# Feed-forward layers that multiply tiles without the norm's column factor, and inner tiles in parts of 8, 8 and 6

## The reference, cut to what matters

```
def _rmsnorm(x, g):
    xf = x.astype(jnp.float32)
    y = xf * lax.rsqrt(jnp.mean(xf * xf, axis=-1, keepdims=True) + EPS)
    return (y * g.astype(jnp.float32)).astype(x.dtype)
...
        h = _rmsnorm(x, p['norm_ffn'][l])
        x = x + (jax.nn.silu(h @ p['w_ffn_gate'][l]) * (h @ p['w_ffn_up'][l])) @ p['w_ffn_down'][l]
    y = _rmsnorm(x, p['norm_final'])
```

## Time and profile before

| | before |
|---|---|
| median of 3 runs | 2166.68 us (2166.18 to 2167.81) |
| the profiled execution | 2165.86 us, span 2164.1 us |
| PE busy | 2062.3 us, 95% of the span |
| PEld busy | 1876.2 us, 87% |
| DVE busy | 879.3 us, 41% |
| ACT busy | 430.5 us, 20% |
| POOL busy | 914.9 us, 42% |
| mean granted TensorE clock | 0.979 of full speed |

### The profile page before, as it was taken

The page is one execution under the profiler, slowest core; times in us unless marked ns, Lnnn a source line. Parts: engine busy times, 40 slices in busy tenths (PEclk is TensorE's granted clock), DMA queues, the critical chain, the costliest instruction groups (busy, mean ns, idle before and its releaser), DMA issues.

```text
span 2164.1 us, 33587 instructions
## 1 busy us (share of the span) xinstructions
PE 2062.3 (95%) x13453; PEld 1876.2 (87%) x13453; DVE 879.3 (41%) x1118; ACT 430.5 (20%) x671; POOL 914.9 (42%) x580
## 2 busy tenths in 40 slices
PE   6999999889999999989999999999899999999997
PEld 5999988789999999989998746547498999999996
DVE  4565645552222001359932356555722322210125
ACT  3242333221111000121212322323201111100011
POOL 4333323154454454555553123223454454455443
PEclk9999999899999999999999999999999999999998
DMA  4121212112222222232232474765822122222222
GB/s 172 59 86 60 85 57 84 43 57 78 73 72 78 78 68 78 81 137 75 84 121 75 142 268 145 258 208 186 297 88 78 59 68 77 78 72 75 78 77 88
DMA packets 82071, 224.35 MB, mean 104 GB/s; under 512 B 6352, under 2 KB 11344, under 8 KB 81232
## 3 DMA queue, kind: packets, MB, share of 16 engines
q1 hardware_dynamic: 73344, 202.94, 27.7%
q10 hardware_dynamic: 8656, 20.39, 2.6%
HBM read 170.06 MB, written 53.25 MB: 103 GB/s over the span
## 4 chain that ended last, share of the span: by engine, by line
PE 84%; DVE 8%; DMA 3%; ACT 3%; issue 1%; POOL 1%; DVEq 0%; SPq 0%; ACTq 0%; POOLq 0%
PE psd L210 11%; PE psd L214 11%; PE psd L215 11%; PE psd L211 11%; PE psd L217 11%; PE psd L216 11%; DVE ntmp L284 2%; PE psm L389 2%; PE psm L1314 2%; PE psd L1210 1%; PE psd L1199 1%; DMA c_s<-CsB 1%; PE psd L1136 1%; DMA CsB<-st_c 1%; PE psm L1299 1%
## 5 line engine op out<-in xcount | busy, mean ns | idle before, releaser
L1897 POOL CAST whi<-wraw 128x1024 fp32r<-128x1024 f32 x223 | 236.1, 1059 | 916.6 <-PE psd L217 486.7
L1899 POOL TENSOR_TENSOR wlo<-wraw,whi 128x1024 fp32r<-128x1024 f32 x223 | 540.6, 2424 | 17.9
L210 PE MATMUL psd<-xh,whi 128*128 128x320 f32 x1280 | 406.3, 317 | 19.9 <-ACT xh L257 14.1
L214 PE MATMUL psd<-xl,whi 128*128 128x320 f32 x1280 | 402.7, 315 | 9.5 <-POOL xl L292 7.5
L211 PE MATMUL psd<-xh,whi 128*128 128x320 f32 x1280 | 398.8, 312 | 0.0
L215 PE MATMUL psd<-xl,whi 128*128 128x320 f32 x1280 | 398.8, 312 | 0.0
L216 PE MATMUL psd<-xh,wlo 128*128 128x320 f32 x1280 | 398.5, 311 | 0.0
L217 PE MATMUL psd<-xh,wlo 128*128 128x320 f32 x1280 | 398.3, 311 | 0.0
L210 PEld LDWEIGHTS psd<-xh,whi 128*128 128x128 f32 x1280 | 243.2, 190 | 24.3 <-issue 23.6
L214 PEld LDWEIGHTS psd<-xl,whi 128*128 128x128 f32 x1280 | 242.9, 190 | 17.9 <-POOL xl L292 13.1
L211 PEld LDWEIGHTS psd<-xh,whi 128*128 128x128 f32 x1280 | 243.5, 190 | 0.8 <-issue 0.2
(11 more groups left out here) (378 smaller groups left out, 2902.8 us busy)
## 6 DMA issues: line engine op xcount, KB each, us to landing
wraw<-w SPq DMA_DIRECT2D x224, 512.0 KB, 3.3
CsA<-st_c SPq DMA_DIRECT2D x7, 1024.0 KB, 6.2
CsB<-st_c SPq DMA_DIRECT2D x7, 1024.0 KB, 8.8
c_s<-CsA SPq DMA_DIRECT2D x7, 1024.0 KB, 6.0
c_s<-CsB SPq DMA_DIRECT2D x7, 1024.0 KB, 8.8
z_kept<-zb ACTq DMA_DIRECT2D x16, 320.0 KB, 2.2
ztp<-st_c SPq DMA_DIRECT2D x5, 1024.0 KB, 7.8
CsC<-st_c SPq DMA_DIRECT2D x5, 1024.0 KB, 8.2
```

The source lines that it names most:

```text
L210: pe.matmul(o0, wh, x0, start=st, stop=False)
L214: pe.matmul(o0, wh, l0, start=False, stop=False)
L1897: pool.tensor_copy(whi[s][:], wraw[s][:]).then_inc(w_high, 1)
L1899: pool.tensor_tensor(wlo[s][:], wraw[s][:], whi[s][:].bitcast(F32), ALU.subtract).then_inc(w_split, 1)
```

## The change

The column factor `rstd` is no longer applied ahead of the two feed-forward layers. `Norm` gets a mode `raw` (used by `norm1` and `norm3`): as soon as a residual tile is there, ACT writes gain times `xT` as the high part, and DVE makes the low part (`low_raw`) right behind the residual add. PE starts the first gate unit from these, and makes the norm's sum over partitions between that unit's fourth and fifth row tile, into `psm` instead of a `psd` accumulator. DVE now reads the gate's accumulator and multiplies it by `rstd` (into `ffg`, which is `ntmp`), ACT takes Silu from there, DVE multiplies the result by `rstd` once more, and then by the up unit's accumulator as before. The inner tiles come in parts of 8, 8 and 6, so that they and the operand tiles fit into `ah` and `al`: in layer 0 the operand lies in `ah[0:8]`, `al[8:16]` and the inner tiles in `ah[8:16]`, `al[0:8]`; in layer 1 the operand stays in `xh`, `xl`. Down units are as many as before, 16 of 8 row tiles and 8 of 6, but those of 8 no longer share an accumulator two by two, so there are 8 residual adds more in each layer. POOL has no part in the two norms any more. DVE waits for the last head's state stores (`a_out`, `b_out`) ahead of the first residual of out0, and ACT for the store from `CsF` ahead of `norm3`.

```diff
...
-FF_PARTS = (16, 6)
+FF_PARTS = (8, 8, 6)
...
         ntmp = [sb(f"ntmp{s}", [P, T], at=n0) for s in range(4)]
+        ffg = ntmp[0:2]
...
+                    if self.raw is not None:
+                        a.activation(self.raw[0][:, k, :], xT[:, k, :], ACT.Copy,
+                                     scale=par[:, self.gain + k:self.gain + k + 1]).then_inc(self.hi_done, 1)
                     if k >= 2:
                         a.wait_ge(self.acc_done, k)
                     a.activation(sq[k % 2][:], xT[:, k, :], ACT.Square).then_inc(self.sq_done, 1)
                 a.wait_ge(self.sum_done, 1)
-                a.activation(two(rstd[:]), psd[self.g % 2][:, :, 0:HT], ACT.Ln, bias=eps,
+                o = psd[self.g % 2][:, :, 0:HT] if self.raw is None else psm[:, 0:2, 0:HT]
+                a.activation(two(rstd[:]), o, ACT.Ln, bias=eps,
                              scale=1.0 / D).then_inc(self.std_done, 1)
                 a.wait_ge(self.std_done, 1)
                 a.activation(rstd[:], rstd[:], ACT.Exp, scale=-0.5).then_inc(self.std_done, 1)
+                if self.raw is not None:
+                    return
                 a.sem_inc(evac[self.g % 2], 1)
                 if self.final:
                     return
...
+            def low_raw(self, v, k):
+
+                if self.raw is None:
+                    return
+                v.wait_ge(self.hi_done, k + 1)
+                one = lambda x: x[:, bass.ds(k, 1), :].rearrange("p a c -> p (a c)")
+                v.scalar_tensor_tensor(one(self.raw[1]), one(xT), par[:, bass.ds(self.gain + k, 1)],
+                                       one(self.raw[0]).bitcast(F32), ALU.mult, ALU.subtract)\
+                    .then_inc(self.lo_done[0], 1)
 
             def begin(self, v):
...
+                if self.raw is not None:
+                    return self.lo_done[0], k + 1
                 return self.lo_done[k % 2], k // 2 + 1
 
             def pe(self, p):
-                o = psd[self.g % 2]
+                o = psd[self.g % 2] if self.raw is None else psm
                 p.wait_ge(self.acc_done, KD)
...
+        raw1 = ah[:, 0:KD, :], al[:, KD:CI, :]
+        norm1 = Norm("n1", PAR["ffn"], G_N1, U_FF0, lambda k: left(G_OUT0 + k), raw=raw1)
+        raw3 = xh, xl
+        norm3 = Norm("n3", PAR["ffn"] + 8, G_N3, U_FF1, lambda k: left(G_DN1 + k), raw=raw3)
...
                 x = xT[:, bass.ds(2 * i + s, 1), :].rearrange("p a (c d) -> p (a c) d", c=2)
                 v.tensor_tensor(x, x, psd[(g0 + s) % 2][:, :, 0:HT], ALU.add).then_inc(evac[(g0 + s) % 2], 1)
                 if norm is not None:
+                    norm.low_raw(v, 2 * i + s)
                     norm.add(v, 2 * i + s, s)
...
-        def pe_down(pe, u0, g0, nu, nk, ready, ready_at):
+        def pe_down(pe, u0, g0, h, nk, ready, ready_at):
 
             for j in range(2):
-                for q in range(nu):
-                    pe_dense(pe, (u0 + nu * j + q, 0), (g0 + j, 0), ah, al, k0=q * KD, nk=nk, first=q == 0,
-                             last=q == nu - 1,
-                             ready=(lambda k: (ready, ready_at + q * KD + k)) if j == 0 and ready is not None else None)
+                pe_dense(pe, (u0 + j, 0), (g0 + j, 0), *h, nk=nk,
+                         ready=(lambda k: (ready, ready_at + k)) if j == 0 else None)
             with pe.Fori(1, KD // 2) as i:
                 for j in range(2):
-                    for q in range(nu):
-                        pe_dense(pe, (u0 + nu * j + q, nu * i), (g0 + j, i), ah, al, k0=q * KD, nk=nk, first=q == 0,
-                                 last=q == nu - 1)
+                    pe_dense(pe, (u0 + j, i), (g0 + j, i), *h, nk=nk)
...
             def act(self, a):
-                for f, before, u, g, nu in self.parts():
+                for f, before, u, g in self.parts():
                     with a.Fori(0, f // 2) as i:
                         for s in range(2):
                             gg = g + 2 * s
-                            a.wait_ge(pe_unit, u + 4 * i + 2 * s + 1)
-                            a.activation(two(ffs[s][:]), psd[gg % 2][:, :, 0:HT], ACT.Silu).then_inc(evac[gg % 2], 1)
+                            a.wait_ge(evac[gg % 2], gg // 2 + 2 * i + 1)
+                            a.activation(ffs[s][:], ffg[s][:], ACT.Silu).then_inc(self.silu, 1)
                             a.wait_ge(evac[(gg + 1) % 2], (gg + 1) // 2 + 2 * i + 1)
                             if s == 0:
                                 a.wait_ge(pe_unit, u)
-                            a.activation(ah[:, bass.ds(2 * i + s, 1), :].rearrange("p a c -> p (a c)"), fft[s][:],
+                            a.activation(self.h[0][:, bass.ds(2 * i + s, 1), :].rearrange("p a c -> p (a c)"), fft[s][:],
                                          ACT.Copy).then_inc(self.hi, 1)
...
             def vec(self, v):
-                for f, before, u, g, nu in self.parts():
+                v.wait_ge(self.norm.std_done, 2)
+                for f, before, u, g in self.parts():
                     with v.Fori(0, f // 2) as i:
                         for s in range(2):
-                            gg = g + 2 * s
-                            v.wait_ge(evac[gg % 2], gg // 2 + 2 * i + 1)
+                            gg, n = g + 2 * s, before + 2 * i + s
+                            v.wait_ge(pe_unit, u + 4 * i + 2 * s + 1)
+                            v.tensor_tensor(two(ffg[s][:]), psd[gg % 2][:, :, 0:HT], two(rstd[:]), ALU.mult)\
+                                .then_inc(evac[gg % 2], 1)
+                            v.wait_ge(self.silu, n + 1)
+                            v.tensor_tensor(ffs[s][:], ffs[s][:], rstd[:], ALU.mult).then_inc(self.scaled, 1)
+                            v.wait_ge(self.scaled, n + 1)
                             v.wait_ge(pe_unit, u + 4 * i + 2 * s + 2)
                             v.tensor_tensor(two(fft[s][:]), two(ffs[s][:]), psd[(gg + 1) % 2][:, :, 0:HT],
                                             ALU.mult).then_inc(evac[(gg + 1) % 2], 1)
-                            v.wait_ge(self.hi, before + 2 * i + s + 1)
+                            v.wait_ge(self.hi, n + 1)
                             one = lambda x: x[:, bass.ds(2 * i + s, 1), :].rearrange("p a c -> p (a c)")
-                            v.tensor_tensor(one(al), fft[s][:], one(ah).bitcast(F32), ALU.subtract)\
+                            v.tensor_tensor(one(self.h[1]), fft[s][:], one(self.h[0]).bitcast(F32), ALU.subtract)\
                                 .then_inc(self.lo, 1)
-                    vec_residual(v, (u + 2 * f, nu), g + 2 * f, self.after if before else None)
+                    vec_residual(v, (u + 2 * f, 1), g + 2 * f, self.after if before + f == sum(FF_PARTS) else None)
...
             def pe(self, pe):
-                for f, before, u, g, nu in self.parts():
+                for f, before, u, g in self.parts():
                     for j in range(4):
-                        pe_dense(pe, (u + j, 0), (g + j, 0), xh, xl,
-                                 ready=self.norm.ready if before == 0 and j == 0 else None,
-                                 ready_high=self.norm.ready_high if before == 0 and j == 0 else None)
+                        first = before == 0 and j == 0
+                        pe_dense(pe, (u + j, 0), (g + j, 0), *self.x,
+                                 ready=self.norm.ready if first else None,
+                                 ready_high=self.norm.ready_high if first else None,
+                                 between=(lambda: self.norm.pe(pe)) if first else None)
                     with pe.Fori(1, f // 2) as i:
                         for j in range(4):
-                            pe_dense(pe, (u + j, 2 * i), (g + j, 2 * i), xh, xl)
-                    pe_down(pe, u + 2 * f, g + 2 * f, nu, min(f, KD), self.lo, before + 1)
...
-        ffn0 = FeedForward("ff0", U_FF0, G_FF0, norm1, norm2)
-        ffn1 = FeedForward("ff1", U_FF1, G_FF1, norm3, normf)
+                            pe_dense(pe, (u + j, 2 * i), (g + j, 2 * i), *self.x)
+                    pe_down(pe, u + 2 * f, g + 2 * f, self.h, f, self.lo, before + 1)
+
+        ffn0 = FeedForward("ff0", U_FF0, G_FF0, norm1, norm2, raw1, (ah[:, KD:CI, :], al[:, 0:KD, :]))
+        ffn1 = FeedForward("ff1", U_FF1, G_FF1, norm3, normf, raw3, (ah[:, 0:KD, :], al[:, 0:KD, :]))
...
-            splits(2, U_FF0 + 2)
-            norm1.pool(pool)
-            splits(U_FF0 + 2, U_UP1 + 2)
+            splits(2, U_UP1 + 2)
...
-            splits(U_DN1 + 2, U_FF1 + 2)
-            norm3.pool(pool)
-            splits(U_FF1 + 2, N_UNITS)
+            splits(U_DN1 + 2, N_UNITS)
...
+            a.wait_ge(mlstm.cst["F"], 16 * USES.count("F"))
             norm3.act(a)
...
             low(7, 8)
+            v.wait_ge(a_out, 32 * H)
+            v.wait_ge(b_out, 32 * H)
             vec_residual(v, (U_OUT0, 1), G_OUT0, norm1)
-            norm1.vec(v)
             ffn0.vec(v)
...
```

(37 more changed lines are left out.)

6 lines of the change are left out of this document (3 added, 3 removed).

## The result

| | before | changed |
|---|---|---|
| median, runs taken together | 2166.43 us (4 runs, 2161.24 to 2167.81) | 2141.61 us (4 runs, 2140.73 to 2142.07) |
| ratio, 95% interval | | 0.9889 (0.9872 to 0.9906) |
| the profiled execution | 2165.86 us, span 2164.1 | 2142.07 us, span 2139.9 |

The account below looks back on a forecast made before the run. PE, busy 95% of the span, was taken as the bound, so only its stalls give time. Span 2164.1 - 22.7 - 1.2 = 2140.2, plus 1.8 outside it 2142.0, and 0.8 to the median: 2142.8 us, range 2139.4 to 2149.

Parts of the forecast that it names:

- The two norms: At `norm1` and `norm3`, 20.76 us between POOL's casts shrinks to 9.43, giving back 11.3 us each, 22.7 us together.
- The reserves: In the new first unit nothing comes late; the last square has the smallest reserve, 1.0 us, the low part 3.8 us.
- The clock: Through both norms PE no longer idles, so full speed, clock 1.00; the gain is within the norms' 22.7 us.
- The inner tiles: In the feed-forward inner tiles DVE's added multiply, taken as 2.50 us, stays covered by 14.08 us of units; cost 0.
- Parts of 8: At a part's down units the last low part comes 1.7 us early; the part of 6 keeps 0.2 us; cost 0.
- The operand's place: Layer 0's gate and up units, reading `ah`/`al`, gain between 0 and 2.3 us; half was taken, 1.2 us.
- The sum: Whole kernel: the span falls to 2140.2 us, the profiled execution to 2142.0, the median to 2142.8.
- Slower by DVE's order: Inner tiles: PE's release of the gate accumulator waits in DVE's program; at 15 us per tile 2184 us; chance 0.06.
- DVE late over out0: Over out0, DVE's tiles reach 7.7 us, passing the last square's reserve by some 4 us: 2147 us; chance 0.09.
- Waits at the ends of the parts of 8: A last low part 2.7 us later costs 1.0 us at four such ends, 9.4 us in all: 2152; chance 0.08.
- No change by weights: At the norms the stall moves to the second unit's weights, which PE asks for 11 us sooner: 2166 us; chance 0.04.

Follow-up runs that it names:

- sum_first: The changed kernel with the norm's sum behind the first unit's first row tile instead of its fourth; one time, 2143.67 us.
- sum_ahead: The changed kernel with the norm's sum put back ahead of the first unit; 2143.93 us, ratio 0.9900.
- chain4: The changed kernel with four more DVE multiplies in each of two places of every inner tile, results unchanged; one time, 2146.12 us.
- chain5: The changed kernel with five more DVE multiplies in each of two places of every inner tile, results unchanged; one time, 2243.57 us.
- parts: The kernel before with only the inner tiles' parts changed, from 16 and 6 to 8, 8 and 6; 2166.19 us, ratio 0.9998.
- layer1_only: The changed kernel with layer 0's old norm back, its operand in `xh` and `xl`, parts of 8, 8 and 6 kept; 2152.78 us, ratio 0.9944.
- place: The kernel before with parts of 8, 8 and 6 and both layers' feed-forward operand written to `ah[0:8]`, `al[8:16]`; 2165.12 us, ratio 0.9989.
- chain1: The changed kernel with one more DVE multiply in each of two places of every inner tile, results unchanged; 2143.34 us, ratio 0.9891.
- xl64: The changed kernel with `xl` and every buffer behind it 64 bytes further along a partition; 2136.06 us, ratio 0.9854, and again 2136.96 us, ratio 0.9875.

## Why the prediction was right, step by step

- **The two norms** (22.7 forecast, 23.2 measured): the mechanism was right, and the size was 0.5 us short. The 9.43 us that had to stay were 9.15 and 9.20. I had added 0.23 us for the change of kind behind the sum to four full distances of 0.54. The rows show that the last f32 matmul is followed after 0.30, not 0.54, and that the 0.39 behind it makes up for it: sum and change together cost 2.16 us (9.20 - 7.04 at `norm3`). The other 0.05 at `norm1` is its unit, shorter by the operand's place.
- **The reserves.** ACT's timeline of the changed kernel has the last square at

```profile
466.24 0.72 ACT L250 ACTIVATE sq<-xT 128x640 f32<-128x640 f32 x1
```

It ends at 466.96 and is wanted at 469.01, the third row of the sum. So the reserve is 2.05 us. `sum_first` and `sum_ahead`, three and four row tiles of 0.87 earlier, agree to about 0.1: there the square is 0.45 and 1.32 us late. I gave 1.0, because I held the square against the start of the sum. It cost nothing.
- **The clock**: as forecast, 1.00 through both norms. What the lower clock had cost is part of the 11.6 per norm; it wasn't measured apart.
- **The inner tiles** (0 forecast, 0 measured). The new multiply takes 2.71 us beside POOL; 2.50 was taken. It begins at 475.41 and ends at 478.12. POOL's timeline beside it:

```profile
475.03 2.40 POOL L1926 TENSOR_TENSOR wlo<-wraw,whi 128x1024 fp32r<-128x1024 f32 x1
```

This subtraction ends at 477.43, the multiply 0.69 later, about one undisturbed multiply. The low part's subtraction in `chain4` and `chain5` also ends 0.68 behind POOL's, whether it takes 2.29 or 2.95 us. By the Trainium skill ("SBUF — State Buffer", "Who interferes with whom") a VectorE operation with two SBUF inputs and a GpSimd operation that reads SBUF exclude each other for a whole instruction; the traces agree, by these 0.68 to 0.69 us and by the 0.735 us of an added multiply while POOL stands idle.
- **Parts of 8** (0 forecast): `parts` and the stages agree. The 0.2 us wait of the part of 6 remains.
- **The operand's place** (1.2 forecast): the mechanism was there, the size only half. For `layer1_only` and `place` it is 2.3 us in layer 0, the upper end of my term. A further 0.3 us came from the down units of layer 0's part of 6, which run at 145.6 ns in every trace here but that of before; I had counted that one exception as evidence against the gain, and so took the middle. Why that one stretch was slow stays open; the 0.3 us need not be the change's, since other stretches at the fast offset were slow in single profiles too (last section), and in before's own layer 1 the part of 6 came at 145.5 ns (5.24 us a unit, against 5.28 in layer 0). By the Trainium skill ("SBUF — State Buffer", "Who interferes with whom") PE has read ports of its own, which would have made this term 0; measured, it is 2.3.
- **The sum**: the profiled execution gained 2.1 us more than forecast in the stages named (0.5 in the norms, 1.1 + 0.3 by the place, 0.26 in layer 1's mixer, which varies), lost 1.9 us ahead of the first norm, most of it in a stretch that varies by itself, and has 0.4 us more outside its span than the 1.8 that I took. That the forecast came within 1.2 us of the median is partly luck.
- **The rivals.** Slower by DVE's order: the mechanism is real (`chain5`), its point lies at two units, and the change leaves DVE 5.3 us short of it per tile. DVE late over out0: not in the trace, its five undisturbed units take 35.19 us as before. Waits at the ends of the parts of 8: none. No change by weights: PE waits for none at either norm.

## What to carry to other kernels

A factor that belongs to the columns of an operand need not stand ahead of a product: at the evacuation it costs time on an engine that has some, and the tensor engine starts from what is already there. Before such a move, add up the chain of the engine that takes the work against the length of the units it serves: below that length added work cost nothing here (`chain4`), above it every tile paid the difference (`chain5`). And read an edit's effect from the stages it touches: two stretches of unchanged code moved this kernel's time by more than the sum's place or the operand's.

## What was not expected of the hardware

At a granted clock of 1.00, matmuls of 128x320 that take a high and a low tile in turn come every 146.7 or 145.5 ns. In the fourteen profiles, but for the feed-forward layers of `chain5`, where DVE sets the pace, every stretch of whole units whose two tiles lie a multiple of 128 bytes apart was slow. Where they lie 64 bytes over a multiple, the stretches were fast, but for five: the down units of a part of 6 in layer 0 of the kernel before and in layer 1 of `chain1`, layer 1's down projection in `sum_first`, and the first down units of layer 1 in both profiles of `xl64`. So the offset goes with the distance in most stretches and doesn't decide it in all. Only these two offsets were tried, and what lies behind them, and what makes the five slow, stays open. It is 4.4 us of some 2144 for one line of code.
